# Nine row buffers become eight, and a ring of weight chunks keeps eight places instead of six

## The reference

```
q = (xt @ w_q).reshape(T, 8, 2, 128)            # 8 heads
s = einsum('thpd,hpnd->thpn', q, sub_keys)      # 128 keys on each side
... top 16 of each side, then the top 16 of the 256 sums, a softmax over them
uc = take(u_tab, ic, axis=0)                    # 128 rows of u for each token
vc = take(v_tab, ic, axis=0)                    # and the same 128 rows of v
act = gelu(einsum('cd,ckd->ck', xc, uc))
out = einsum('ck,ckd->cd', gates * act, vc)
```

## Time and profile before

| | us |
|---|---|
| three runs | 2637.63, 2638.46, 2640.79 |
| median | 2638.46 |
| profiled execution | 2644.09 |
| its span, first to last instruction | 2641.9 |
| PE busy | 2152.5 (81%) |
| DVE busy | 1362.0 (52%) |
| ACT busy | 633.0 (24%) |
| POOL busy | 494.1 (19%) |
| moved by DMA | 1053.60 MB, mean 399 GB/s |

### The profile page before, as it was taken

One profiled execution on the slowest core, in us unless ns is written; L12 is line 12 of the kernel. 1 busy time (PEld: TensorE's weight loads), 2 busy tenths in 40 slices (PEclk: granted clock), 3 DMA queues, 4 the chain that ended last, 5 costly groups with the idle time before them and its releaser, 6 DMA issues.

```text
span 2641.9 us, 33067 instructions
## 1 busy us (share of the span) xinstructions
PE 2152.5 (81%) x12087; PEld 958.9 (36%) x12087; DVE 1362.0 (52%) x3702; ACT 633.0 (24%) x1521; POOL 494.1 (19%) x534
## 2 busy tenths in 40 slices
PE   8999999999999998998755579578588687565557
PEld 6633333333333334994421123125123235121112
DVE  2422222122222122777677777874675875587754
ACT  0411111111111111342222242431232442232212
POOL 1000000000000000013333333332333332243331
PEclk9999999999999999998987789789799899797778
DMA  7999999999999998859999999999999999999995
GB/s 258 359 405 429 429 428 428 429 426 430 429 429 428 428 428 354 297 188 411 420 419 420 420 416 407 420 419 417 420 412 417 401 406 416 419 399 421 421 421 226
DMA packets 134408, 1053.60 MB, mean 399 GB/s; under 512 B 15600, under 2 KB 16024, under 8 KB 44176
## 3 DMA queue, kind: packets, MB, share of 16 engines
q0 software_dynamic: 75104, 540.07, 49.6%
q1 hardware_dynamic: 59184, 511.98, 46.9%
HBM read 1050.92 MB, written 2.63 MB: 399 GB/s over the span
## 4 chain that ended last, share of the span: by engine, by line
PE 41%; DMA 39%; DVE 14%; ACT 3%; issue 2%; POOL 1%; SPq 0%; DVEq 0%; ACTq 0%
DMA big<-in_uv,small 22%; PE ps L884 15%; DMA big<-in_w_gate_up 14%; PE ps L1351 7%; DVE big L2477 5%; PE ps L1047 3%; PE ps L1155 3%; DMA ring<-in_uv,small 2%; PE ps L926 2%; PE ps L1169 2%; PE ps L867 1%; PE ps L712 1%; ACT small L1871 1%; DVE small L2410 1%; DVE small L2407 1%
## 5 line engine op out<-in xcount | busy, mean ns | idle before, releaser
L1351 PE MATMUL ps<-big,small 64*64 64x512 f32 x3776 | 593.7, 740 | 390.5 <-ACT small L1871 390.1
L2695 POOL DMA_INDIRECT big<-in_uv,small x473 | 446.9, 945 | 1989.5 <-DVE small L2452 1112.9
L2477 DVE SCALAR_TENSOR_TENSOR big<-big,ps 128x1024 f32<-128x1024 f32 x473 | 569.5, 1217 | 267.1 <-DMA big<-in_uv,small 266.5
L884 PE MATMUL ps<-big 128*64 128x512 f32 x2304 | 525.5, 599 | 25.9 <-DMA big<-in_w_gate_up 23.6
L1351 PEld LDWEIGHTS ps<-big,small 64*64 64x64 f32 x3776 | 148.3, 156 | 758.7 <-ACT small L1871 568.4
L884 PEld LDWEIGHTS ps<-big 128*64 128x64 f32 x2304 | 155.9, 137 | 332.8 <-issue 288.3
L1871 ACT ACTIVATE small<-small 128x64 f32<-128x64 f32 x512 | 150.3, 340 | 299.5 <-DVE small L2504 251.8
L2154 DVE COPY big<-ps 128x512 f32<-128x512 f32 x32 | 22.1, 691 | 382.0 <-PE ps L884 382.0
L1865 ACT ACTIVATE small<-small 128x2 f32<-128x2 f32 (+1 forms) x225 | 51.7, 230 | 592.9 <-DVE big L2477 549.7
L2140 DVE TENSOR_TENSOR big<-ps,big 128x256 f32<-128x256 f32 x64 | 27.2, 424 | 299.6 <-PE ps L908 299.6
L1047 PEld LDWEIGHTS ps<-hs,ring 128*128 128x128 f32 x1152 | 131.0, 192 | 17.2 <-issue 15.4
(11 more groups left out here) (403 smaller groups left out, 2313.5 us busy)
## 6 DMA issues: line engine op xcount, KB each, us to landing
big<-in_w_gate_up SPq DMA_DIRECT2D x80, 2048.0 KB, 22.7
big<-in_w_down SPq DMA_DIRECT2D x64, 2048.0 KB, 24.2
ring<-in_w_gate_up SPq DMA_DIRECT2D x32, 2048.0 KB, 26.1
hs<-in_w_gate_up SPq DMA_DIRECT2D x16, 2048.0 KB, 26.1
ring<-in_peer_w_q SPq DMA_DIRECT2D x48, 512.0 KB, 12.6
ring<-in_ple_w_gate SPq DMA_DIRECT2D x22, 512.0 KB, 16.1
ring<-in_w_in SPq DMA_DIRECT2D x16, 512.0 KB, 7.7
ring<-in_a_w_in SPq DMA_DIRECT2D x16, 512.0 KB, 4.8
```

What stands on the lines that cost most here:

```text
L884: last = pe.matmul(ps[side * CAP:(side + 1) * CAP, bank + b, :], o, w[:, at:at + BANK], start=start, stop=stop, skip_group_check=True)
L1351: last = pe.matmul(ps[tokens_ if by_halves else at, bank, :], diagonal(k)[tokens_, :], rows(k)[tokens_, D + z * BANK:D + (z + 1) * BANK], ...
L2477: ins = dve.scalar_tensor_tensor(r, r, 1.0, tok, op0=ALU.mult, op1=ALU.mult, accum_out=dots[:, k % PICKS:k % PICKS + 1])
L2695: pool.indirect_dma_start(out=rows(k), out_offset=None, in_=io[f"uv{n // UNITS}"], in_offset=bass.IndirectOffsetOnAxis(ap=rows_at[:, at:at ...
```

## The change

The ring of the chain takes all eight places, and there is no ninth row buffer.

```diff
-RING, CHAIN_RING = 8, 6
+RING, CHAIN_RING = 8, 8
...
-ROWS, MORE_ROWS, MORE_AT = 8, 1, 168
+ROWS, MORE_ROWS, MORE_AT = 8, 0, 168
```

## The result

| | before | changed |
|---|---|---|
| median of 16 runs each, us | 2640.66 | 2644.26 |
| lowest and highest | 2637.62, 2645.04 | 2640.18, 2649.68 |
| ratio to before | | 1.0015 [1.0008, 1.0022] |
| profiled execution, us | 2644.09 | 2640.84 |
| first to last product of DVE in the gather half, two profiles each | 1437.8, 1436.4 | 1439.3, 1439.1 |

The change costs 0.15%, that is 2640.66 x 0.0015 = 4.0 us, with 2.1 and 5.8 us as the ends of the interval. The predicted cost was 10.9 us: the sign is right, the size is nearly three times too large. The predicted time (2649.4) lies 5 us above the measured one, and part of that distance is hidden, as the median of before came out 2.2 us higher in 16 runs than in the three that the forecast started from. By the bound of 0.2% the ratio counts as no change, which had a chance of 0.19.

What follows compares the result with a forecast made beforehand. DMA's rate was taken as the bound, with idle in gaps where an engine sets the pace; seven terms for the lost row buffer sum to 10.9 us, ring 0: 2638.46 + 10.9 = 2649.4 us, range 2641.5 to 2656 (own range 2643.7 to 2654.5).

Steps and rivals of the forecast that it cites:

- the bound of 0.2%: Changes under 0.2% (5.3 us) count as none: slower begins at 2643.7 us, faster ends at 2633.2; no change had 0.19.
- the account of bytes: Whole kernel: the change adds and removes no byte, so only DMA's idle time and its place can differ.
- the first gap: Stretch 1602 to 1630, its later part: the gather at 1621.35 loses the ninth buffer, 1.5 us.
- once for each gap, however long it is: In each gap DMA stops one row earlier with eight buffers, so the end comes up to 2.49 us later.
- The five later terms: Losses at 1898 to 1943 (1.5 us), 1982 to 2010 (1.9), 2063 to 2133 (2.5), 2292 to 2356 (2.5), 2380 to 2606 (0.5).
- the heavy gap: Stretch 2063 to 2133: DMA already starves with nine buffers, so a full row is lost, 2.5 us.
- the twin: 1602 to 1630 and 1982 to 2010, same work on eight and nine buffers: the ninth is worth 1.9 us.
- the ring: Two more weight places: eight loads issued near 1345, 2.49 us later from there, given back later; net 0, low end -6.7.
- The stretch at 1982: Sharpest sign: 385 to 395 GB/s at 1982 to 2010; the prediction is wrong if it keeps 417 on eight buffers.
- 2063 and 2292: Sign: one row more lost in each of these two gaps, 2.5 us each.
- The first rival: No change, 2638 to 2642 us: PE's release of two rows at a time stops DMA, not the buffer count; chance 0.19.
- The rule that spoke against the change costing anything: Skill's estimate of 4.4 us per 1 MB gather: two outstanding rows would do, the sum falling towards the first rival's 2640.

Runs made afterwards that it cites:

- e6: The changed kernel with two more row buffers from gather 304 on, ten in all; 2641.08 us, ratio 1.0002 to before.
- e9: The changed kernel with one more row buffer from gather 304 on, nine in all; 2639.97 us, ratio 0.9996 to before.
- e12: The kernel before, but with ten row buffers from gather 80 on and a ring of four; 2641.10 us, ratio 0.9999 to before.

## Why the prediction was right in sign and wrong in size

**Right: the account of bytes.** Queues, bytes and the rate between gaps (418, 420, 421) are as before, and idle time rises by 2.45 us where the gather part rises by 2.15.

**Right: the first gap.** 1.75 us for 1.5 (2.1 with the further profiles). Here the ninth buffer was first filled, and the row is lost.

**Wrong: "once for each gap, however long it is".** This is the step that failed. The prediction said: "At a gap's start DVE is waiting for rows, at its end again. In between DMA may run ahead by what the buffers hold." The first sentence doesn't mean that DMA starts from nothing. DVE waits for the slowest of 16 engines, and 1.6 to 2.1 MB of later rows are there before the gap. The buffer was lost already, in this stock, and a later gap gains as much as before. The five later terms of 1.5, 1.9, 2.5, 2.5 and 0.5 measure 0.2, 0.45, 0.5, 0.1 and 0.25: 8.9 us forecast, 1.5 measured. The price itself was sound at the same spread: e6 and e9, which enter the heavy gap with the spread of eight buffers, gain 2.5 and 2.9 us there for each buffer. What the prediction had no term for is that the ninth buffer widens the spread, from 5.0 to 8.7 us before the heavy gap, and by the table above a gap entered with a wider spread idles longer, by about what the buffer gives.

**Wrong: the twin.** 1602 to 1630 and 1982 to 2010 were read as the same work on eight and nine buffers, 2.1 and 0.3 us lost. On eight buffers both, they still give 387 and 416 GB/s (380 and 403 in the second profile). Most of the difference is not the buffer's. e12, with ten buffers in the first stretch, has hardly any idle time there (0.4 us), so more buffers do fill it; what else sets the two apart was not tried. Two stretches with equal work differ also in what lies before them, and one pair is no experiment.

**Missing: the end.** What the engines are ahead is useless at the last row. One buffer less gives 1.4 us back there.

**Right: the ring.** Eight chunks near 1341, phase 0 longer by 344.75 - 342.4 = 2.35 us for 2.5 forecast, given back later, and net nothing. Over all runs phase 0 takes 339.2 to 339.7 us with four places, 341.4 to 343.0 with six and 344.2 to 345.5 with eight. PE's waits for `in_peer_w_q` (5.8 us in five) are gone, and no time with them; with a ring of four over 100 us of such waits cost nothing either.

**Signs.** The stretch at 1982, named as the sharpest sign, kept 416 GB/s (403 in the second profile) for 385 to 395, and no row more is lost at 2063 and 2292. By the prediction's own words ("wrong if the stretch at 1982 keeps 417 on eight buffers") its account of the gaps is wrong, though its range for the time holds. The other signs came: eight issues, the later end of phase 0, and no wait of DVE for rows in the heavy gap. Landing times did shrink by about 3 us (issue to last piece, end of phase 1: 22.3 to 18.8; end of phase 3: 15.5 to 12.9). POOL's wait for PE before its gathers hardly grew, 879.9 to 883.4 us in all. The first rival (no change) had the better time, but its mechanism, two rows freed at a time by PE, isn't supported: in e12 PE frees rows in the same pairs at 1602, and with ten buffers DMA idles 0.4 us there.

**The rule that spoke against the change costing anything.** An estimate by the Trainium skill (DMA: Bandwidth & Descriptors, "Anatomy of one DMA — SWDGE (gpsimd) path") had given 4.4 us for a 1 MB gather. Two outstanding rows as enough was concluded from it, and that doesn't hold here: seven buffers cost 10 us more than eight. The gathers of these traces wait behind others, so what one takes with nothing queued before it no run shows.

**What stays open.** Why one DMA engine lags with ten buffers and which it is, as the records don't number them, and what sets the spread besides the buffers (eight with a ring of four had 6.1 us at the end of phase 1, but 1.5 at ticks 22 to 24 of phase 2). Why the step from eight to seven costs 10 us and that from nine to eight 4; that the spread can't shrink further fits, but no run isolates it. And about 2 us of the median's 4.0 that the gather parts of two profiles don't show.

## What to carry to other kernels

A consumer that waits for a transfer doesn't prove that nothing is there: compare the bytes moved with the bytes taken at that moment, because a transfer spread over 16 engines ends with the slowest, and the others may be rows ahead. In this kernel a buffer more or less counts once, where the stock ahead is first built or lost, and not once for each stall, as more buffers came with a wider spread of the engines; part of it is stranded at the end of the stream. The worth of one more buffer is also not constant (seven to eight 10 us, eight to nine 4, nine to ten none that shows, of 2640), so measure it at the count in question.

## What the runs showed of the hardware

- The 16 pieces of a 1 MB gather land over 1.5 to 12 us. With seven, eight, nine and ten buffers the mean at ticks 22 to 24 of phase 2 is 2.8, 5.0, 8.7 and 11.5 us; a limit of five gathers under way leaves 8.5, and a ring of four beside eight buffers has 1.5.
- With ten buffers (e6) fifteen pieces of a row land within 2.4 us in phase 3 and the last 4.5 us after them; at the end one engine alone is busy for 5 us. With eight buffers the last piece comes 0.4 to 0.7 us after the 15th there.
- With the same spread of 5 us at its start the gap of 2063 idles 6.1, 3.2 and 1.1 us with eight, nine and ten buffers.
- 86 us of PE waiting for weights beside a saturated DMA cost nothing that shows: ratios of 1.0018 and 1.0015, with 0.001 on either side.
